# Gate chunks run ahead of the branch chunks while the convolution norm is computed

## The reference

```python
u = rms_norm(h, g_pre_mix)
z_pool, v_conv, g_conv, gate_a, gate_b = split(u @ w_in)
y_a = pool(z_pool) @ w_grp * scale @ w_pool_out
c   = depthwise_conv31(v_conv * sigmoid(g_conv)) + b_dw
y_b = silu(layer_norm(c, conv_ln_g, conv_ln_b)) @ w_conv_out
m   = sigmoid(gate_a) * y_a + sigmoid(gate_b) * y_b
h   = h + rms_norm(m @ w_o, g_post_mix)
```

## Time and profile before

| | us |
|---|---|
| median of 3 runs | 2169.06 (2168.93 to 2170.14) |
| the profiled execution, own time | 2166.54 |
| its span | 2164.7 |
| TensorE matmul busy | 2061.9 (95%) |
| VectorE busy | 1384.6 (64%) |
| ScalarE busy | 933.3 (43%) |

### The profile page before, as it was taken

One profiled execution on the slowest core, in us unless ns is written; L12 is line 12 of the kernel. 1 busy time (PEld: TensorE's weight loads), 2 busy tenths in 40 slices (PEclk: granted clock), 3 DMA queues, 4 the chain that ended last, 5 costly groups with the idle time before them and its releaser, 6 DMA issues.

```text
span 2164.7 us, 36901 instructions
## 1 busy us (share of the span) xinstructions
PE 2061.9 (95%) x14348; PEld 1874.7 (87%) x14348; DVE 1384.6 (64%) x1911; ACT 933.3 (43%) x1389; POOL 26.4 (1%) x53
## 2 busy tenths in 40 slices
PE   5999988998999999799997999999999999999998
PEld 2789878768999988799997999889889989989986
DVE  5366667676677866888997555465545545545555
ACT  3354444335544553433344334444434434433443
POOL 0000000000000000000000000000000000000000
PEclk9999999998999999899998999999999999999999
DMA  9976877784567555245443554545555555555553
GB/s 382 407 288 260 324 292 297 268 310 156 195 230 270 221 195 213 98 176 176 174 174 137 176 193 176 193 158 188 191 192 184 190 192 182 191 195 181 187 195 136
DMA packets 64208, 462.30 MB, mean 214 GB/s; under 512 B 7120, under 2 KB 7632, under 8 KB 8176
## 3 DMA queue, kind: packets, MB, share of 16 engines
q1 hardware_dynamic: 57152, 410.49, 51.4%
q0 software_dynamic: 6960, 50.46, 6.3%
HBM read 458.83 MB, written 2.10 MB: 213 GB/s over the span
## 4 chain that ended last, share of the span: by engine, by line
PE 67%; DVE 7%; ACT 2%; issue 1%; DMA 0%; DVEq 0%; SPq 0%; ACTq 0%
PE ps L472 22%; PE ps L473 22%; PE ps L474 22%; DVE w_lo L1624 3%; DVE area L1660 1%; ACT w_hi L1107 1%; PE ps L514 1%; DVE st L1644 1%; ACT sc L1357 0%; ACT sc L1363 0%; DVE X L2084 0%; DVE grow L2182 0%; DVE area L2182 0%; DMA raw<-in_stream 0%; DVE csil L2033 0%
## 5 line engine op out<-in xcount | busy, mean ns | idle before, releaser
L1624 DVE TENSOR_TENSOR w_lo<-raw,w_hi 128x1024 fp32r<-128x1024 f32 x642 | 758.5, 1221 | 406.0 <-ACT w_hi L1107 402.5
L472 PE MATMUL ps<-a_hi,w_lo 128*128 128x256 f32 (+1 forms) x2912 | 831.7, 286 | 12.7 <-DVE w_lo L1624 6.7
L1107 ACT CAST w_hi<-raw 128x1024 fp32r<-128x1024 f32 (+1 forms) x642 | 640.8, 1047 | 456.7 <-PE ps L474 451.0
L473 PE MATMUL ps<-a_lo,w_hi 128*128 128x256 f32 (+1 forms) x2912 | 827.0, 284 | 0.0
L474 PE MATMUL ps<-a_hi,w_hi 128*128 128x256 f32 (+1 forms) x2912 | 825.5, 283 | 0.0
L472 PEld LDWEIGHTS ps<-a_hi,w_lo 128*128 128x128 f32 x2912 | 555.5, 191 | 40.2 <-issue 31.4
L474 PEld LDWEIGHTS ps<-a_hi,w_hi 128*128 128x128 f32 x2912 | 555.6, 191 | 0.0
L473 PEld LDWEIGHTS ps<-a_lo,w_hi 128*128 128x128 f32 x2912 | 553.0, 190 | 0.8 <-issue 0.5
L472 PE MATMUL ps<-w_hi,y_lo 128*128 128x512 f32 x720 | 283.2, 393 | 7.4 <-DVE w_lo L1624 4.8
L473 PE MATMUL ps<-w_lo,y_hi 128*128 128x512 f32 x720 | 281.5, 391 | 0.0
L474 PE MATMUL ps<-w_hi,y_hi 128*128 128x512 f32 x720 | 281.3, 391 | 0.0
(11 more groups left out here) (274 smaller groups left out, 2076.1 us busy)
## 6 DMA issues: line engine op xcount, KB each, us to landing
raw<-in_stream SPq DMA_DIRECT2D x331, 1024.0 KB, 4.8
area<-in_ada SPq DMA_DIRECT2D x46, 1024.0 KB, 7.8
area<-in_ada POOLq DMA_DIRECT2D x40, 1024.0 KB, 5.2
grow<-in_ada SPq DMA_DIRECT2D x10, 1024.0 KB, 7.5
grow<-in_rows POOLq DMA_DIRECT2D x4, 1024.0 KB, 6.0
area<-in_rows POOLq DMA_DIRECT2D x4, 1024.0 KB, 6.4
X<-in_x SPq DMA_DIRECT2D x1, 2048.0 KB, 7.5
out<-X SPq DMA_DIRECT2D x4, 512.0 KB, 2.6
```

The costliest lines, as they stand in the source:

```text
L472: pe.matmul(o, w[1], a[0], start=first, stop=False, skip_group_check=shared)
L473: pe.matmul(o, w[0], a[1], start=False, stop=False, skip_group_check=shared)
L1107: ac.copy(to, raw[:, bass.ds((g % RAW) * CH + h * n, n)]).then_inc(hi_ready, 1)
L1624: ve.tensor_tensor(to, raw[:, bass.ds((g % RAW) * CH + h * n, n)], hi.bitcast(F32), ALU.subtract).then_inc(lo_ready, 1)
```

## The change

Three gate pairs (six chunks) now stand in the stream and in TensorE's order ahead of the first branches, followed by their six branch chunks; the loop begins with the fourth pair. The results of the six gates are kept in free parts of `grow` (`gate_buf`), so the load of the next gain row into it waits for six finished branches. The mean's sum over the eight tiles is gathered on VectorE in `msum`, one addition per round of the mixing loop, and TensorE does one matmul with ones on it, after three quarters of the first gate. The norm works on pairs of tiles: VectorE multiplies four pairs by the reciprocal, ScalarE applies gain and bias (`gained`), ScalarE takes the tanh of a pair, VectorE multiplies a pair. VectorE's pool subtractions move to the end of the norm, ScalarE's into two groups of four. The splits of the chunks are placed between these steps (`ahead_split`), some in halves.

```diff
+AHEAD = 3
+
+
+def gate_chunk(i, b):
+
+    return B2_GATE + (2 * i if isinstance(i, int) and i < AHEAD else 4 * i) + b
+
+
+def branch_chunk(i, b):
+
+    return B2_GATE + (2 * AHEAD + 2 * i if isinstance(i, int) and i < AHEAD else 4 * i + 2) + b
...
-        mu = grow[:, 0:T]
+        mu, msum = grow[:, 0:T], grow[:, T:2 * T]
...
-        def cn_buf(k):
-
-            return (sc[:, 2 * T:3 * T], sc[:, 3 * T:4 * T], zs[:, :], th[:, 0:T])[k % 4]
+        def cn_buf(p):
+
+            return sc[:, p % 2 * 2 * T:(p % 2 + 1) * 2 * T]
+
+        def gate_buf(i, b):
+
+            at = 2 * (i + 1) * T if isinstance(i, int) and i < AHEAD else None
+            return sc[:, b * T:(b + 1) * T] if at is None else grow[:, at + b * T:at + (b + 1) * T]
...
-            pool.wait_ge(cn_l, CONV)
+            pool.wait_ge(gt_done, 2 * AHEAD)
...
-            gate_b(0, 0)
+            gate_b(0, 0, range(3))
+            pe.wait_ge(cm_pre, 1)
+            pe.matmul(bank(6), ones[:, :], msum, start=True, stop=True).then_inc(cm_ps, 1)
+            gate_b(0, 0, (3,))
+            gate_b(0, 1)
+            gate_b(1, 0, range(2))
             pe.wait_ge(cm_fold, 1)
             pe.matmul(bank(6, T), ones[:, :], zs[:, :], start=True, stop=True).then_inc(cm_acc, 1)
-            gate_b(0, 1)
-            pool_part(0, 0, True)
-            pool_part(0, 1, True)
-            conv_part(0, 0, True)
-            conv_part(0, 1, True)
-            with pe.Fori(1, KT // 2) as i:
+            gate_b(1, 0, (2, 3))
+            gate_b(1, 1)
+            for b in range(2):
+                gate_b(2, b)
+            pool_part(0, 0)
+            pool_part(0, 1)
+            conv_part(0, 0)
+            conv_part(0, 1)
+            for i in range(1, AHEAD):
+                for b in range(2):
+                    pool_part(i, b)
+                    conv_part(i, b)
+            with pe.Fori(AHEAD, KT // 2) as i:
...
+            def gained(p):
+                ac.wait_ge(cn_r, p + 1)
+                for k in (2 * p, 2 * p + 1):
+                    c = conv_out[:, k * T:(k + 1) * T]
+                    ac.activation(c, c, ACT.Identity, scale=v("conv_ln_g", k), bias=v("conv_ln_b", k)).then_inc(cn_y, 1)
+
+            def gain_tanh(p):
+                ac.wait_ge(cn_y, 2 * p + 2)
+                if p >= 2:
+                    ac.wait_ge(cn_mul, p - 1)
+                ac.activation(cn_buf(p), conv_out[:, 2 * p * T:(2 * p + 2) * T], ACT.Tanh, scale=0.5).then_inc(cn_tanh, 1)
+
+            def conv_hi(p):
+                ac.wait_ge(cn_mul, p + 1)
+                ac.activation(y_hi[:, 2 * p * T:(2 * p + 2) * T], conv_out[:, 2 * p * T:(2 * p + 2) * T],
+                              ACT.Copy, scale=0.5).then_inc(cn_h, 1)
+
+            ac.wait_ge(weights_used, B2_GRP + 1)
+            after(B2_GRP, B2_GRP)
+            pooled(range(4))
+            gate_b(0, 0)
+            for i in range(CONV // 2):
+                squared(i)
+            pooled(range(4, CONV))
+            gate_b(0, 1)
             rstd("conv")
-            for k in range(CONV + 2):
-                if k < CONV:
-                    ac.wait_ge(cn_y, k + 1)
-                    ac.activation(cn_buf(k), conv_out[:, k * T:(k + 1) * T], ACT.Tanh, scale=0.5).then_inc(cn_tanh, 1)
-                if k >= 2:
-                    ac.wait_ge(cn_mul, k - 1)
-                    ac.activation(y_hi[:, (k - 2) * T:(k - 1) * T], conv_out[:, (k - 2) * T:(k - 1) * T],
-                                  ACT.Copy, scale=0.5).then_inc(cn_h, 1)
-                if k == 3:
-                    gate_b(0, 1, True)
-            branches(0, 0)
-            branches(0, 1)
-            with ac.Fori(1, KT // 2 - 1) as i:
+            gate_b(1, 0)
+            gained(0)
+            gained(1)
+            gain_tanh(0)
+            gained(2)
+            gain_tanh(1)
+            gained(3)
+            gate_b(1, 1)
+            gain_tanh(2)
+            conv_hi(0)
+            gain_tanh(3)
+            conv_hi(1)
+            gate_b(2, 0)
+            conv_hi(2)
+            conv_hi(3)
+            gate_b(2, 1)
...
+            def sum_tiles(j):
+
+                c = conv_out[:, j * T:(j + 1) * T]
+                own.link(ve.tensor_tensor(msum, conv_out[:, 0:T] if j == 1 else msum, c, ALU.add))
+
             for j in range(CONV):
                 g = B2_MIX + MIX * j
                 if j:
                     ve.wait_ge(cv_done, j)
                 after(g, g)
+                if j >= 2:
+                    sum_tiles(j - 1)
...
-                if j < CONV - 1:
-                    after(g + 4, g)
+                after(g + 4, g)
...
+            ve.wait_ge(cv_done, CONV)
+            sum_tiles(CONV - 1)
+            ve.sem_inc(cm_pre, 1)
+            ahead_split(1)
             ve.wait_ge(cm_ps, 1)
             own.link(ve.tensor_scalar(mu, bank(6), 1.0 / (CONV * P), None, ALU.mult))
             for i in range(CONV // 2):
-                s = tiles(conv_out[:, 2 * i * T:(2 * i + 2) * T], 2)
+                s = tiles(conv_pair(i), 2)
                 ve.tensor_tensor(s, s, over_tokens(mu, 2), ALU.subtract).then_inc(cm_cent, 1)
-                if i:
-                    add_square(i - 1, rs[:, :], cm_sq, cm_sum)
-            add_square(CONV // 2 - 1, rs[:, :], cm_sq, cm_sum)
-            ve.wait_ge(cm_sum, CONV // 2)
+            ahead_split(2, (0,))
+            for i in range(1, CONV // 2):
+                square_sum(i)
+            ve.wait_ge(cm_sum, CONV // 2 - 1)
             ve.tensor_tensor(zs[:, :], rs[:, 0:T], rs[:, T:2 * T], ALU.add).then_inc(cm_fold, 1)
-            after(B2_GATE, B2_GATE)
+            ahead_split(2, (1,))
             ve.wait_ge(cm_acc, 1)
-            rstd("conv", rs[:, 0:T], bank(6, T), CONV * P, 1e-5)
-            for k in range(CONV + 2):
-                if k < CONV:
-                    c = conv_out[:, k * T:(k + 1) * T]
-                    own.link(ve.tensor_tensor(c, c, rs[:, 0:T], ALU.mult))
-                    ve.tensor_scalar(c, c, v("conv_ln_g", k), v("conv_ln_b", k), ALU.mult, ALU.add)\
-                        .then_inc(cn_y, 1)
-                if 1 <= k <= CONV:
-                    c = conv_out[:, (k - 1) * T:k * T]
-                    ve.wait_ge(cn_tanh, k)
-                    ve.scalar_tensor_tensor(out=c, in0=cn_buf(k - 1), scalar=1.0, in1=c, op0=ALU.add,
-                                            op1=ALU.mult).then_inc(cn_mul, 1)
-                if k >= 2:
-                    s = slice((k - 2) * T, (k - 1) * T)
-                    ve.wait_ge(cn_h, k - 1)
-                    ve.scalar_tensor_tensor(out=y_lo[:, s], in0=conv_out[:, s], scalar=0.5,
-                                            in1=y_hi[:, s].bitcast(F32), op0=ALU.mult, op1=ALU.subtract)\
-                        .then_inc(cn_l, 1)
-                if k == 3:
-                    after(B2_GATE + 1, B2_GATE + 1)
+            ve.tensor_scalar(rs[:, 0:T], bank(6, T), 1.0 / (CONV * P), 1e-5, ALU.mult, ALU.add).then_inc(ln_var, 1)
+            ahead_split(3, (0,))
+            ve.wait_ge(ln_std, NORM["conv"] + 1)
+            own.link(ve.reciprocal(rs[:, 0:T], rs[:, 0:T]))
+            ahead_split(3, (1,))
+            for p in range(CONV // 2):
+                s = tiles(conv_pair(p), 2)
+                ve.tensor_tensor(s, s, over_tokens(rs[:, 0:T], 2), ALU.mult).then_inc(cn_r, 1)
+            ahead_split(4)
+            for p in range(CONV // 2):
+                ve.wait_ge(cn_tanh, p + 1)
+                ve.scalar_tensor_tensor(out=conv_pair(p), in0=cn_buf(p), scalar=1.0, in1=conv_pair(p),
+                                        op0=ALU.add, op1=ALU.mult).then_inc(cn_mul, 1)
+                if p == 1:
+                    ahead_split(5)
+            pooled()
+            conv_lo(0)
+            conv_lo(1)
+            ahead_split(6)
+            conv_lo(2)
+            conv_lo(3)
+            ahead_split(7)
...
-    parts.append(np.concatenate([gb.reshape(KT // 2, 2, P, CH), branch], axis=1).reshape(2 * KT, P, CH))
+    gate = gb.reshape(KT // 2, 2, P, CH)
+    parts.extend([t[:AHEAD].reshape(2 * AHEAD, P, CH) for t in (gate, branch)])
+    parts.append(np.concatenate([gate[AHEAD:], branch[AHEAD:]], axis=1).reshape(-1, P, CH))
     parts.append(by_block(np.asarray(i["w_o_2"][0])))
```

More of the change, by code:

```diff
@@ L1000, in _, with gate_b, pool_part @@
             o.then_inc(weights_used, 1)
[L1002 to L1015, removed]
+            def gate_b(i, b, quarters=range(4)):
+                for k in quarters:
+                    if k == 0:
+                        pe.wait_ge(gt_tanh, KT + 2 * i + b - 1)
+                    if k % 2 == 0:
+                        half(gate_chunk(i, b), k // 2)
+                    o = blocks((B2_GATE + b) % 2, bank(3 + b), a_ops, range(4 * k, 4 * k + 4), k == 0, k == 3)
+                    if k == 3:
+                        o.then_inc(weights_used, 1)
+            def pool_part(i, b):
+                half(branch_chunk(i, b), 0)
+                if isinstance(i, int) and i == 0:
```

(31 more changed lines are left out.)

63 lines of the change are left out of this document (30 added, 33 removed).

## The result

The changed kernel takes **2149.24 us** (median of four, 2147.51 to 2156.57) against 2169.60 in the same comparison: a ratio of 0.9912, 95% interval 0.9889 to 0.9936. The forecast was 2148.9. The profiled execution took 2147.51 us, its span is 2145.6 us.

A forecast was written before the change was run, and what follows sets the result against it. TensorE was taken as the bound. Removing 20.5 us of waits and slow clock plus 2.9 of work, less 3.2 of new waits, gains about 20.2: 2169.06 - 20.2 = 2148.9 us, range 2145.5 to 2154.5.

The forecast's parts named there:

- 20.5 us of waits and slow clock: From pool-group matmuls to first loop gate: 47.1 us, of which 26.6 is work at full clock, the rest removable.
- the table rule: Rival at ScalarE's table loads: a switch costs 2.66 us, not 1.28; 2.6 us more, 2151.5 us; chance 0.03.
- two clock falls: Rival at the last two new TensorE waits: clock falls, 2.1 us each; one or two give 2151.0 to 2153.1; chance 0.16.
- The mean: VectorE adds the eight tiles, saving TensorE 2.9 us; sum ready at 1138.2, TensorE arrives 1138.9, no wait.
- The variance and the reciprocal: Fold ends at 1148.6, covered by gates, 5.1 us wait gone; reciprocal 1154.7, chunk 3's second half split 1156.0.
- The new waits: TensorE waits at chunks 2, 3, 4, 6, 7: 0.1 + 0.5 + 0.7 + 1.35 + 0.6 = 3.2 us.
- Gain and bias on ScalarE: In the norm, eight Identity steps taken at 0.50 us each; this kernel's own Identity row gave 0.48, 3.9 for eight.
- The norm that stays slow: Rival in the norm: pairs don't help, it ends at 1184.6 instead of 1174.5; 10 us lost, 2159; chance 0.05.
- No wait came back elsewhere: Rival at the six chunk splits: each queues 3 us behind norm work, so no change; chance 0.03.
- The gain row's load: On the GpSimd queue, moves behind the sixth finished branch, near 1208 instead of 1173; its reader stands over 110 us later.

The follow-up runs named there:

- both forms undone: The change with gain and bias on VectorE and norm steps tile by tile, order kept: 423.00 us between the mixing-loop and w_o table loads, against 420.02.
- single tiles: The change with every norm step on 256 instead of 512 columns: 420.70 us between the mixing-loop and w_o table loads, against 420.02; median 2146.96 us.

## Why the prediction was right

**The size.** The sum was 20.5 us of waits and slow clock, 2.9 of work, less 3.2 of new waits: 20.2. The stretch gave 20.35. That the median, 2149.24, came within 0.4 us of the 2148.9 forecast is luck in part: the four times behind it spread over 9 us. One slip of the working is in the range: its high end of 2154.5 is said to take in the table rule and two clock falls, which it does for either by itself (2151.5 and 2153.1) but not for both (2.6 + 4.2 on 2148.9 is 2155.7).

**The mean.** Right: the sum was ready at 1138.2 of the old time scale, as worked out, and TensorE didn't wait for it. The run with the sum on TensorE puts its work at 2.7 us, not 2.9.

**The variance and the reciprocal.** Right to 0.15 us: fold 1148.7 against 1148.6, table load ended 1152.4 against 1152.5, reciprocal 1154.6 against 1154.7, chunk 3's second half 1155.9 against 1156.0.

**The new waits.** The term that was mis-sized: 3.2 us were forecast in five places. The profile counts 1.8 in four (0.12, 0.53, 0.82, 0.34), but it counts from the shown end of a matmul, while the sum went from start to start. Counted that way (the wait, plus 0.28 for the last matmul, less its 0.12) chunk 2 cost nothing (0.1 said), chunk 3 0.28 (0.5), chunk 4 0.69 (0.7), chunk 6 0.98 (1.35), chunk 7 0.50 (0.6), and each of the four restarts has a first matmul that takes about 0.1 longer: 2.85 in all. The largest miss is at chunk 6: its split was ready at 1171.9 instead of 1172.2. About 0.17 of that lies in the last two pair products, 1.21 us for both (1166.49 to 1167.70) where twice 0.69 were taken. The rest may be ScalarE's 512-column steps, which start 0.52 us apart (two squares in 1.15) though each is shown with 0.63; no run parts this out. With the 2.7 us of the tile sum, 20.5 + 2.7 - 2.85 = 20.35, what was measured; that it meets to the hundredth is chance, since 20.5 is itself a difference of readings.

**Gain and bias on ScalarE.** The 0.50 us taken for one was right, and it was read from this kernel's own Identity row; the plain tanh would have given about 0.3 a start (0.39 as shown, less the 0.1 by which ScalarE's steps overlap). Moving it was worth 1.4 us.

**The rivals.** The table switch costs 1.28 us and no more. The tanh starts at 1155.51, 0.01 us behind the load that began at 1154.22, in the changed kernel too, and ahead of the root's load ScalarE stands idle for 0.02 us (1152.47 to 1152.49). The Trainium skill, "ScalarE: Activation LUTs", section "What ACT_TABLE_LOAD costs", gives 2.66 us for a switch; no load here followed by ready work shows that. The clock didn't fall, in any of three profiles. The two last waits were 0.82 and 0.34 us instead of 1.35 and 0.6, less than the forecast's 1.95 us together; with 1.85 and 0.35 there (gain and bias on VectorE) it held too, in one profile. The norm that stays slow was built, and the loss of 9.6 us is what that rival said. It gave the wrong place (the first branch, instead of gate 5 in the norm), and its cause, pairs that don't help, is not the one: order is. No wait came back elsewhere, and the part behind the stretch stayed at 819.8 us. The gain row's load was issued at 1210.3, or 1209.0 of the old scale (near 1208 said).

## What to carry to other kernels

A long chain between two engines that can't be shortened can be covered by matmuls that don't depend on it; here the cover was worth about its own length, in idle time and in slow clock, where the chain ended later than the cover (the third pair of gates, 11.4 us of work, gave 10.4). It pays to write the queue of the engine that works on the chain so that no step waits for its own predecessor's trip through the other engine: do one step for all tiles, then the next (6.6 of the 9.6 us here). What is left is read from the idle rows of that engine; work without a due time, moved there, gave another 1.8 us.

## What the runs showed of the hardware

The granted clock held over a wait of 1.85 us ahead of the first branch (gain and bias on VectorE). After one of 2.12 us at the same place it fell (both forms undone). In the kernel before it fell after 2.6. The first window is of the one, the other two of the other; the columns are those of the windows above:

```profile
1178.00:1184.00 6.00, 5.65 (x45) 5.45 (x46) 4.55 (x5) 0.45 (x1) 0.00 (x0) 1.00 0.58 186
...
1180.00:1182.00 2.00, 1.95 (x14) 1.96 (x15) 2.00 (x4) 0.23 (x1) 0.00 (x0) 0.83 0.00 0
1182.00:1184.00 2.00, 2.00 (x11) 2.00 (x11) 2.00 (x4) 0.00 (x0) 0.00 (x0) 0.50 0.75 221
```

But the length of a wait doesn't decide this by itself. About 90 us behind the stretch, among matmuls of another kind, TensorE waits 1.68 us. In the changed kernel the clock falls behind that wait; in the kernel with single tiles, behind the same wait, it doesn't. First the wait and a window of the change, then those of single tiles:

```profile
1414.65 1.61 PE L532 MATMUL ps<-con,X 128*128 128x128 f32 x8 [1.68 <-DVE X L2393]
1415.50:1422.30 6.80, 5.55 (x26) 5.18 (x26) 4.22 (x10) 2.87 (x8) 0.00 (x0) 0.50 0.33 135
...
1423.59 1.32 PE L532 MATMUL ps<-con,X 128*128 128x128 f32 x8 [1.68 <-DVE X L2401]
1424.50:1431.30 6.80, 5.25 (x46) 5.04 (x45) 4.16 (x10) 3.68 (x11) 0.00 (x0) 1.00 0.33 137
```

The clock fell there in thirteen of the fourteen profiles of this case, and again after a wait of 1.9 us some 20 us later; single tiles is the one in which it fell at neither. The part behind the stretch took 816.07 us in that profile and 819.03 to 820.19 in the others. What else decides isn't shown. So the stretches of the two kernels with waits of 1.85 and 2.12 us, one profile each, may differ by a fall of the clock from one execution to the next.

The stretch repeated within 0.02 us in three profiles of the same kernel, while the 900 us ahead of it took 905.8, 912.1 and 908.8 us. Times of whole runs of one kernel spread by up to 12 us (2163.5 to 2176.0 for the kernel before in one comparison), and a change of 2 us is better read from the stage it is in.
